# A two-block network in one kernel: a modulation unit moved to the second half of the wide projection, the rotary partner by DMA, channel sums pre-added on VectorE

## The reference

```python
c_act = jax.nn.silu(c)
for l in range(DEPTH_2):
    mod = c_act @ w_ada[l] + b_ada[l]
    shift, scale, gate = jnp.split(mod, 3, axis=-1)
    h = _rmsnorm(x, norm_g[l]) * (1.0 + scale[:, None, :]) + shift[:, None, :]
    z = h @ w_in[l]
    (f_x, f_g, na_q, na_k, na_v, na_g, r_q, r_k, r_v, r_g,
     cv_a, cv_b, cv_g) = jnp.split(z, N_IN_PIECES, axis=-1)
    ...                       # Fourier mix, neighbourhood attention, retention, convolution
    y = jnp.concatenate([o_fft, o_na, o_ret, o_cv], axis=-1) @ w_out[l]
    x = x + gate[:, None, :] * y
```

## Time and profile before

| | |
|---|---|
| median of 3 runs | 2106.51 us (2105.36 to 2107.66) |
| profiled run | 2108.31 us |
| its span, first to last instruction | 2106.5 us |
| TensorE busy | 2054.5 us, 98% |
| VectorE busy | 1749.3 us, 83% |
| ScalarE busy | 1193.3 us, 57% |
| mean granted clock of TensorE | 0.990 |

### The profile page before, as it was taken

How to read it: one execution, slowest core, us unless ns; L and a number is a source line. 1 busy time by engine, 2 the same in 40 slices (tenths; PEclk the granted TensorE clock), 3 DMA queues, 4 the chain that set the end, 5 groups by cost and what they waited for, 6 DMA issues and landing times.

```text
span 2106.5 us, 42698 instructions
## 1 busy us (share of the span) xinstructions
PE 2054.5 (98%) x19052; PEld 1658.5 (79%) x19052; DVE 1749.3 (83%) x1660; ACT 1193.3 (57%) x1065; POOL 39.0 (2%) x39
## 2 busy tenths in 40 slices
PE   8999999999999999999999999999999899999998
PEld 7889888888889946555555568888888788888887
DVE  7885787988887798999999989999558689995655
ACT  5554544444444577888878864455544444565543
POOL 0002300000000000000000000000000000000000
PEclk9999999999999999999999999999999999999999
DMA  8854487889888788999999978864448778744552
GB/s 303 317 200 159 174 317 257 294 309 335 319 304 309 287 302 340 420 420 420 420 418 416 404 276 310 288 242 168 154 170 302 279 278 311 251 166 145 180 201 100
DMA packets 95574, 593.25 MB, mean 282 GB/s; under 512 B 10648, under 2 KB 10808, under 8 KB 36640
## 3 DMA queue, kind: packets, MB, share of 16 engines
q1 hardware_dynamic: 94768, 583.73, 73.7%
q0 software_dynamic: 624, 6.80, 0.9%
HBM read 588.39 MB, written 2.10 MB: 280 GB/s over the span
## 4 chain that ended last, share of the span: by engine, by line
PE 70%; DVE 15%; DMA 8%; ACT 3%; issue 3%; DVEq 0%; POOL 0%; ACTq 0%; POOLq 0%
PE GB L2167 52%; DVE w_lo L1241 6%; PE GB L2586 4%; PE MB L2586 3%; DVE W L1241 3%; DMA W<-w_ada 2%; ACT w_hi L622 2%; DMA Z<-w_ada 2%; DMA raw<-w_up 1%; DVE Z L1221 1%; DVE W L1221 1%; DMA raw<-w_gate 1%; DMA Z<-w_up 1%; PE MB L2755 1%; DMA Z<-w_down 1%
## 5 line engine op out<-in xcount | busy, mean ns | idle before, releaser
L622 ACT ACTIVATE w_hi<-raw 128x2048 f16<-128x2048 f32 x295 | 563.1, 1910 | 703.6 <-PE GB L2167 681.6
L1241 DVE SCALAR_TENSOR_TENSOR w_lo<-raw,w_hi 128x2048 f16<-128x2048 f32 x295 | 676.5, 2294 | 254.2 <-ACT w_hi L622 253.0
L2167 PE MATMUL GB<-H,w_hi 128*128 128x256 f16 x4352 | 717.2, 273 | 12.5 <-DVE w_lo L1241 8.9
L2167 PE MATMUL GB<-H,w_lo 128*128 128x256 f16 x2176 | 593.3, 273 | 0.0
L2167 PEld LDWEIGHTS GB<-H,w_hi 128*128 128x128 f16 x4352 | 421.7, 98 | 77.1 <-issue 13.0
L2167 PEld LDWEIGHTS GB<-H,w_lo 128*128 128x128 f16 x2176 | 213.0, 98 | 24.8
L2167 PE MATMUL GB<-w_hi,H 128*128 128x256 f16 x1280 | 210.7, 273 | 0.0
L1221 DVE SCALAR_TENSOR_TENSOR W<-W,SM 128x1024 f32<-128x1024 f32 x120 | 153.8, 1281 | 30.3 <-DMA W<-w_ada 26.9
L2167 PE MATMUL GB<-w_lo,H 128*128 128x256 f16 x640 | 174.4, 273 | 0.0
L2167 PE MATMUL GB<-Z,w_hi 128*128 128x256 f16 x1024 | 169.9, 274 | 3.6 <-DVE w_lo L1241 3.6
L2167 PE MATMUL GB<-W,w_hi 128*128 128x256 f16 x1024 | 168.2, 273 | 3.7 <-DVE w_lo L1241 3.7
(11 more groups left out here) (478 smaller groups left out, 2804.5 us busy)
## 6 DMA issues: line engine op xcount, KB each, us to landing
raw<-w_in SPq DMA_DIRECT2D x144, 1024.0 KB, 5.1
W<-w_ada SPq DMA_DIRECT2D x128, 512.0 KB, 5.7
raw<-w_out SPq DMA_DIRECT2D x48, 1024.0 KB, 5.0
raw<-w_down SPq DMA_DIRECT2D x41, 1024.0 KB, 10.5
raw<-w_gate SPq DMA_DIRECT2D x34, 1024.0 KB, 10.3
raw<-w_up SPq DMA_DIRECT2D x32, 1024.0 KB, 11.8
Z<-w_ada SPq DMA_DIRECT2D x64, 512.0 KB, 5.6
raw<-xattn_wk SPq DMA_DIRECT2D x16, 1024.0 KB, 5.2
```

Source lines behind the costliest of these rows:

```text
L622: act.activation(w, raw_at[r], ACT.Copy, scale=W_SCALE).then_inc(hi_done, 1)
L1241: dve.scalar_tensor_tensor(lo, raw_at[r], W_SCALE, hi, ALU.mult, ALU.subtract).then_inc(raw_taken[r], 1)
L2167: last = pe.matmul(o, a, m, start=first, stop=end and w_part is lo, skip_group_check=True)
```

## The change

**Modulation.** Of the two units in each wide projection the first keeps its place (16 steps between m = 2 and 16). The second, 8 or 11, goes to steps 35 to 46. It uses the slots in `w2` and the sums in `w3`, which attention has left by then; SP waits for attention's last product (`na_o`) ahead of its first transfer. `ada_columns` of the first unit goes from step 17 to 19 and into MB, that of the second from 32 to 50 and into GB; the Fourier parts `f_parts` and `f_last` move from w2 to w1.

**Rotary.** `rotate` and its constant are gone. POOL copies the partner rows (each block of 32 partitions from its neighbour) from Z to one of three buffers in Y, four DMAs of 32 x 512 values for each pair of tiles; the sign goes into the table of sines. VectorE multiplies what has landed there, at the same steps as before.

**Channel sums.** VectorE adds the four channel tiles to one before the product with ones: after the last tap at step 38 for the mean, in the new `conv_squares` at step 42 for the squares. TensorE then has one product in place of four.

```diff
-Z_UNITS = (7, 8, 10, 11)
+Z_UNITS = (7, 10)
...
-    def fast(ph):
-        for m in [2 + 2 * k // 3 for k in range(13)] + list(range(11, 30)):
+    def halves(ph):
+        for m in [2, 2, 3, 4, 4, 5, 6, 6, 7, 8, 8, 9, 10, 12, 14, 16]:
+            put(ph, m)
+        for m in [35, 36, 37, 37, 38, 39, 39, 40, 41, 41, 42, 42, 43, 44, 45, 46]:
             put(ph, m)
...
-        RO = Y[:, 5:7, :]
-        f_parts = w2[:, 0:1024].rearrange("p (a k g n) -> p a k g n", a=TT, k=2, g=4)
-        f_last = w2[:, 1024:1032].rearrange("p (a g) -> p a g", a=TT)
+        RO = [Y[:, 5 + 2 * k:7 + 2 * k, :] for k in range(3)]
+        f_parts = w1[:, 0:1024].rearrange("p (a k g n) -> p a k g n", a=TT, k=2, g=4)
+        f_last = w1[:, 1024:1032].rearrange("p (a g) -> p a g", a=TT)
...
         def ada_bank(u):
-            return MB[:, 0, 0:8] if u in (8, 11) else GB[:, 2, 0:8]
+            return MB[:, 0, 0:8] if u in Z_UNITS else GB[:, 2, 0:8]
...
+            LATE_ROOM = {8 * ADA_STEPS: 4, 11 * ADA_STEPS: 8}
...
                     for step in steps:
+                        if step in LATE_ROOM:
+                            sp.wait_ge(S("na_o"), LATE_ROOM[step])
                         load_ada(step)
...
                 gp.dma_start(W[:, 0:2 * BLK], A["na_rel_bias_2"][l]).then_inc(S("bias_in"), 16)
+                for j in range(4):
+                    for u in range(j % 2 + 1):
+                        gp.wait_ge(bank_free[u], uses[f"z{l}"][u] + 6 + j // 2)
+                    if j == 0:
+                        gp.wait_ge(S("tap"), 4 * TAPS * l + 4)
+                    if j == 3:
+                        gp.wait_ge(S("rotated"), 4 * l + 1)
+                    if l or j:
+                        gp.wait_ge(S("rot"), 64 * (4 * l + j))
+                    for d in range(0, P, DH // 2):
+                        s = d ^ DH // 2
+                        gp.dma_start(RO[j % 3][d:d + DH // 2], Z[s:s + DH // 2, 24 + 2 * j:26 + 2 * j, :]).then_inc(S("rot"), 16)
...
+                def four_to_one(x):
+                    link(dve.tensor_tensor(CU[:, 0:2, 0:T], x[:, 0:2, :], x[:, 2:4, :], ALU.add))
+                    return dve.tensor_tensor(CU[:, 0, 0:T], CU[:, 0, 0:T], CU[:, 1, 0:T], ALU.add)
+
+                def conv_squares():
+                    dve.wait_ge(S("squared"), 2 * l + 1)
+                    dve.wait_ge(S("conv_pe"), 2 * l + 1)
+                    four_to_one(csq).then_inc(S("conv_a"), 1)
...
                         dve.wait_ge(S("tap"), n_taps + 4 * TAPS)
-                        dve.sem_inc(S("conv_a"), 1)
+                        four_to_one(ca).then_inc(S("conv_a"), 1)
...
-                    dve.wait_ge(S("rot"), 4 * l + j + 1)
-                    link(dve.tensor_tensor(RO, GB[:, 2, :].rearrange("p (c t) -> p c t", t=T), sin, ALU.mult))
+                    dve.wait_ge(S("rot"), 64 * (4 * l + j + 1))
+                    ro = RO[j % 3]
+                    link(dve.tensor_tensor(ro, ro, sin, ALU.mult))
...
+                    if m == 42:
+                        conv_squares()
...
                     if c == 0:
                         evicted(pe, l, 3)
+                        pe.wait_ge(ada_mod, 8 + 3 * l)
...
-                def rotate(j):
...
-                def conv_sum(k, src, o):
+                def conv_sum(k, o):
+                    pe.wait_ge(S("conv_a"), 2 * l + k + 1)
...
-                    for c in range(4):
-                        ins = pe.matmul(o, ones[:, :], src[:, c, :], start=c == 0, stop=c == 3)
-                    ins.then_inc(S("conv_pe"), 1)
+                    pe.matmul(o, ones[:, :], CU[:, 0, 0:T], start=True, stop=True).then_inc(S("conv_pe"), 1)
...
-                    if m == 17:
+                    if m == 19:
                         ada_columns(7 + 3 * l)
-                    if m == 32:
-                        pe.wait_ge(S("na_max"), 8 * l + 8)
+                    if m == 50:
+                        pe.wait_ge(S("fft_act"), 7 * l + 7)
                         ada_columns(8 + 3 * l)
-                    for j in nth(m, 27, 2):
-                        rotate(j)
```

More of the change, by code:

```diff
@@ L75, in constants @@
     rope = (t.astype(np.float32)[None, :] * inv[p % half][:, None]).astype(np.float32)
[L76 to L83, removed]
+    out["rope_cos"], out["rope_sin"] = np.cos(rope), np.sin(rope) * np.where(p % DH < half, -1.0, 1.0)[:, None]
     d = t[None, :] - t[:, None]
@@ L165, in ada_plan @@
         put("wo", m)
-    fast("z0")
+    halves("z0")
     for m in [2, 2, 3, 4, 4, 5, 6, 6, 7, 8, 8, 9, 9, 10, 10, 11]:
         put("mix0", m)
-    fast("z1")
+    halves("z1")
     assert count[0] == 12 * ADA_STEPS
@@ L358, in ada_sums @@
             if u in Z_UNITS:
-                return Zf[:, (4 * (u in (8, 11))) * T:(4 * (u in (8, 11)) + 4) * T]
+                return Zf[:, 0:4 * T]
             return SUMS[:, u % 2, :]
@@ L1231, in _ @@
             adds = {("w_in", 22): 0, ("wk", 10): 1, ("wq", 9): 2, ("wv", 3): 3, ("wv", 13): 4, ("wo", 8): 5,
-                    ("z0", 20): 7, ("z0", 33): 8, ("mix0", 14): 9, ("z1", 20): 10, ("z1", 33): 11}
+                    ("z0", 20): 7, ("z0", 51): 8, ("mix0", 14): 9, ("z1", 20): 10, ("z1", 51): 11}
             def split(ph, j, i=0):
@@ L1969, in rotary @@
                     x = Z[:, 24 + 2 * j:26 + 2 * j, :]
-                    dve.wait_ge(S("rot"), 4 * l + j + 1)
-                    link(dve.tensor_tensor(RO, GB[:, 2, :].rearrange("p (c t) -> p c t", t=T), sin, ALU.mult))
+                    dve.wait_ge(S("rot"), 64 * (4 * l + j + 1))
+                    ro = RO[j % 3]
+                    link(dve.tensor_tensor(ro, ro, sin, ALU.mult))
                     link(dve.tensor_tensor(x, x, cos, ALU.mult))
-                    dve.tensor_tensor(x, x, RO, ALU.add).then_inc(S("rotated"), 1)
+                    dve.tensor_tensor(x, x, ro, ALU.add).then_inc(S("rotated"), 1)
                 def decay_sum(c):
@@ L2658, in ret_scores @@
                         pe.wait_ge(S("na_max"), 8 * l + 8)
-                        pe.wait_ge(ada_mod, 9 + 3 * l)
                     else:
@@ L2734, in fft_map @@
                     pe.sem_inc(S("small_mm"), 1)
-                def conv_sum(k, src, o):
+                def conv_sum(k, o):
+                    pe.wait_ge(S("conv_a"), 2 * l + k + 1)
                     if k == 0:
-                        pe.wait_ge(S("conv_a"), l + 1)
                         pe.wait_ge(S("rotated"), 4 * l + 4)
                     else:
-                        pe.wait_ge(S("squared"), 2 * l + 1)
                         pe.wait_ge(S("conv_act"), 2 * l + 1)
-                    for c in range(4):
-                        ins = pe.matmul(o, ones[:, :], src[:, c, :], start=c == 0, stop=c == 3)
-                    ins.then_inc(S("conv_pe"), 1)
+                    pe.matmul(o, ones[:, :], CU[:, 0, 0:T], start=True, stop=True).then_inc(S("conv_pe"), 1)
                 def small(name, x, banks):
@@ L2777, in _ @@
                     if m == 40:
-                        conv_sum(0, ca, GB[:, 2, 0:T])
+                        conv_sum(0, GB[:, 2, 0:T])
                     if m == 43:
-                        conv_sum(1, csq, GB[:, 2, T:2 * T])
+                        conv_sum(1, GB[:, 2, T:2 * T])
                     for a in nth(m, 38, 2, TT):
```

## The result

The changed kernel is slower, and slower than the range allowed for: its median is 2121.45 us (five runs, 2116.41 to 2122.06) beside 2107.66 us for the kernel before in runs interleaved with it. The ratio is 1.0053, 95% interval 1.0033 to 1.0073. The profiled run took 2117.28 us, with a span of 2115.1, against 2108.31 and 2106.5 before. That execution is one of the two fastest of the five (spans 2114.2 to 2119.9), so a span carries a few us of its own; the mean granted clock is 0.983 or 0.984 in all five, where the profiled run of the kernel before has 0.990. So the question is where 8.6 us of span come from when the sum said +0.5.

A forecast was written before the change was run, and what follows sets the result against it. TensorE, busy 98% of the span, was taken as the bound. The terms -7.5 - 5.2 - 2.3 + 1.3 + 2.8 + 7.4 + 3.2 + 0.8 gave +0.5 on 2106.5, so 2107.0 us, range 2101.5 to 2113.

The forecast's parts named there:

- channel sums: TensorE: one matmul pair left of four, 1.30 us saved, four times, -5.2 us.
- Rotations and gone waits: TensorE: four rotations per layer removed, -7.5 us; late w_lo waits at steps 12 and 22 gone, -2.3 us.
- Step 34: ret_scores waits for the fourth rotary, 0.53 us and some 0.1 for the signal; +1.3 us for both layers.
- VectorE at steps 35 to 39: Modulation steps and pre-add make w_lo late for block 39; +1.4 us per layer, +2.8, bounds 1.0 and 2.5.
- VectorE ahead of fft_map: Steps 44 and 45: two modulation steps delay the mirrored weights; TensorE waits 4.4 us, +3.7 per layer, +7.4.
- The clock: Behind fft_map's wait: one fall to half rate per layer, 1.6 us of work lost each, +3.2; bounds 0 and 2 x 2.4.
- The page's rule: Trainium skill's warning that long idle gaps between matmul bursts drop TensorE to half clock; made the fall at fft_map certain.
- Transfers: Moved unit's weights in two w2 slots, steps 39 to 44: some land late for lo(44), VectorE's w_lo; +0.8 us, both layers.
- rival (c): Steps 40 to 43: landings of 7.8 us, not 5.8, delay w_lo of 44; +11.6 us, 2118; chance 0.13.
- rival (d): Rotary partner by POOL's DMAs comes late and rotaries wait; with 32 us, 2 more per layer, 2111; chance 0.04.
- Rival (a): Moved modulation fits in VectorE's idle time, so no wait at fft_map; 2092 us; chance 0.13.
- rival (b): Clock stays up behind fft_map's wait, all else as forecast; 2103.8 us, 2102 with small terms low; chance 0.22.

The follow-up runs named there:

- e5: Changed kernel with units 8 and 11 back in their old place (steps 11 to 29, old buffers); median 2114.94 us, ratio 1.0022 to the kernel before.
- e3: Changed kernel with the modulation steps of 44, 45 and 46 moved to 46, 47 and 48; median 2105.76 us, ratio 0.9989 to the kernel before.
- e2: Changed kernel with fft_map one block later on TensorE, behind block 45, the wait kept; median 2111.02 us, ratio 0.9999 to the kernel before.
- e1: Changed kernel with 19 unused products of a constant filling TensorE's wait ahead of fft_map; median 2106.95 us, ratio 0.9977 to the kernel before.
- e7: e4 with modulation steps of 37 and 38 moved to 35 and 39, fourth rotary at step 33; median 2095.99 us, ratio 0.9926 to the kernel before.
- e4: e3 with the mirrored weights made at the head of step 44 instead of step 45; median 2097.01 us, ratio 0.9932 to the kernel before.
- e6: e5 with the mirrored weights made at the head of step 44 instead of step 45; median 2104.39 us, ratio 0.9963 to the kernel before.
- e8: Changed kernel with only the mirrored weights moved from step 45 to the head of step 44; median 2098.28 us, ratio 0.9937 to the kernel before.

## Why the prediction was wrong, point by point

Between events that all traces have, the kernels compare as follows (us, after less before; z0, then z1). "34" is the start of ret_scores, "pw" the end of the Fourier products at step 48:

| stretch | in the sum, for a layer | measured |
|---|---|---|
| z0 step 3, z1 likewise, to 34 | -4.4 and -4.0 (rotations, gone waits, +0.6) | -4.6 and -4.0 |
| 34 to ret_square_sum | -1.2 (+1.4 at block 39, -2.6 channel sums) | -1.4 and -1.4 |
| ret_square_sum to fft_map | +3.7 | +3.7 and +3.7 |
| fft_map to pw | +1.6 | +6.2 and +6.9 |

The measured columns add up to 9.0, beside 8.6 of span. Only the last row is far from the sum.

- **Rotations and gone waits: right.** The waits ahead of block 12 in z0 and block 22 in both layers are gone. That the sum to step 34 comes out is partly an offset: a wait of 0.71 came in ahead of block 9 of z0 and those ahead of 7 and 11 shrank, from 0.72 to 0.38 and 0.35, though the forecast kept the one at 11 whole. And e5 shows the condition that the prediction took for granted rather than argued: without the moved unit, 2.0 of 3.7 us would have come back at block 33. **Step 34:** idle 0.41 (0.6 forecast).
- **VectorE at steps 35 to 39: right in place, a little large:** 0.99 at block 39 against 1.3. Between the bound of 1.0 and the value taken.
- **VectorE ahead of fft_map: right,** 4.26 against 4.4, and e3 and e5 give its two parts: 1.87 without modulation steps in the way (0.57 of before and the 1.3 by which TensorE comes earlier), 2.39 from the two steps.
- **The clock: the step that failed.** The term was +3.2 for both layers with an upper bound of 4.8; it measured 6.2 + 6.9 = 13.1. The forecast took its price from the fall behind the 2.06 us idle ahead of 272.57, where whole blocks of 128x256 matmuls follow, and read it as the price of a fall. It is the price of that fall with what follows it. Behind this wait stands fft_map, 10.9 us of float32 matmuls of 129 columns in z0, nearly all at half clock, and 11.5 in z1, all of it; the clock came back only once blocks had run for 3.6 us in z0 and 3.8 in z1. e2 puts a block there instead: 6.8 us of half clock in place of 13.6 and 17.1. e1 takes the fall away and keeps the time: 12.3 us of span back. With 13.1 in place of 3.2 the sum gives 2106.5 + 10.4 = 2116.9, beside the measured span of 2115.1. Which property of fft_map's matmuls keeps the clock down (type, columns, or its products of 4 rows) no run isolates.
- **The fall that gave the price doesn't always come.** The wait ahead of that same block is 2.05 or 2.06 us in all ten traces of this case, in code that no edit touches. The clock fell behind it in five (before, e1, e2, e5, e7) and stayed up in five (the changed kernel, e3, e4, e6, e8). In the changed kernel:

```profile
273.27 0.39 PE L2189 MATMUL GB<-Z,w_hi 128*128 128x256 f16 x2 [2.06 <-DVE w_lo L1251]
...
273.27:276.90 3.63, 3.63 (x34) 3.25 (x35) 3.63 (x3) 2.10 (x2) 0.61 (x1) 1.00 0.72 239
```

- **A row of before that was not read** shows that 3.6 us is no upper bound. At z1's start TensorE idles 2.42 us and small float32 matmuls of the norm follow; half clock lasts 6.8 us there, twice as long as at 273. It isn't the same case: in slices of 0.5 us the clock falls 0.4 us into that idle time, so the wait needn't be its cause, and it is up again ahead of the first block at 1683.30, behind 4.6 us of small products. Timeline of TensorE and stretch, both of the kernel before:

```profile
1678.38 1.22 PE L2216 MATMUL MB<-NS,ones 128*128 128x256 f32 x2 [2.42 <-DVE NS L1297]
1679.39 3.62 PE L2190 MATMUL GB<-ones 128*128 128x128 f32 x16
```

```profile
1676.00:1683.00 7.00, 4.62 (x18) 4.16 (x18) 5.62 (x13) 2.60 (x6) 0.00 (x0) 0.52 1.00 394
```

- **The page's rule** (the Trainium skill, "TensorE: Matmul & The Clock Gate", section "Why this matters for your kernels", on long idle gaps): by it the fall was certain at 4.4, and the trace agrees, in both layers, and in e2 again. What it warns of is the fall; the price here, 13.6 and 17.1 us of half clock, is read from the runs alone. The shorter waits (1.87 to 2.05) follow no rule of length alone: in the z phases of e3, e5 and e6 the clock fell behind five of them and stayed up behind three.
- **Transfers, forecast +0.8 and rival (c): nothing of it.** `w_lo` of 44 starts at 1515.29 right behind w_hi, and the moved unit's only waits for `w_ada` are 0.27 and 0.46 us at step 46, behind the mirrored weights; rival (c) falls. (By the forecast's own terms it would have made the kernel slower from a landing of some 6.7 us on, not 6.5.) **The partner by DMA, rival (d): at nothing,** as taken. POOL's 32 issues landed in 1.8 to 5.9 us, median 1.9, and each group was issued as soon as ScalarE had evicted the pair. Rival (a) falls with the 4.26, rival (b) with the 0.53.
- Why e3's and e5's identical waits dropped the clock in one place and not in another stays open. What went before the wait and where in the program it lies were the same in e3's two layers.

The direction of the error was one-sided. Each doubt about the clock was priced at its cheapest example. The bound that should have come from "what if it stays low for all of fft_map" was in the trace of before: 6.39 us of small products there can cost up to as much again in a layer, above the 2.4 allowed, and they cost 4.5 in z0.

## What to carry to other kernels

Where a change makes TensorE wait, look at what follows the wait: with a dense block there the half clock was over in 6.8 us (e2), while fft_map's small float32 products ran at half rate for nearly all their length, and the fall then cost more than the wait itself (6.2 and 6.9 us beside 4.26). Order VectorE's work within a step by who waits for it, awaited results first and filler such as the modulation steps behind them; that was worth about 17 us here (e8's profiled span against the changed kernel's; 1.2% by the two ratios) for one moved call. If a wait can't be avoided, filling it with matmuls whose result is not used kept the clock up in e1 and cost no time, since they fitted into the wait.

## What was not expected of the hardware

- **How long the half clock lasts depends on what runs in it.** 3.4 us in e5 and at 273 in the kernel before, 6.8 us in e2 behind 4.60 and 4.22 us of idle time, 13.6 or 17.1 us when fft_map follows.
- **Identical waits, different outcomes:** behind 1.87 to 2.05 us in the z phases the clock had fallen in z0 of e3 and at all four places of e5, and was up in z1 of e3 and at both places of e6. Behind the 2.06 us ahead of the block at 273 it fell in five traces of ten.
- **Small float32 products can go with either level.** 4.4 us of 128x128 products of a constant held the clock up in e1, fft_map's ran at 1.00 in z1 of e3, and the norm's products at 1679 (L2190 of the kernel before) ran at half clock, which ended at about 1683.2, ahead of the first block. Only fft_map's kept it down for 10 us and more.
- **Small SBUF to SBUF copies by POOL,** four of 64 KB for each pair, land in a median of 1.9 us while VectorE is busy 81.19 of 90 us, and nobody waits for them:

```profile
L615 POOL DMA_DIRECT2D Y<-Z x32: 496/496/515, 1379.2 to 1848.0; - x32
...
DMA to landing us min/median/max: 1.8/1.9/5.9
```
